# Stick-breaking attention weights as sigmoid(z) times a scanned product of sigmoid(-z), with the mask of a step ahead of the scan of the step before

## What is computed

```python
def sb_attend(q, k, v, q_pos, k_pos):
    z = jnp.einsum('bqhd,bkhd->bhqk', q, k).astype(jnp.float32) * SB_SCALE
    visible = (k_pos[None, :] < q_pos[:, None])[None, None]
    log_skip = jnp.where(visible, jax.nn.log_sigmoid(-z), 0.0)
    between = lax.cumsum(log_skip, axis=3, reverse=True) - log_skip
    weight = jnp.where(visible, jnp.exp(jax.nn.log_sigmoid(z) + between), 0.0)
    return jnp.einsum('bhqk,bkhd->bqhd', weight.astype(v.dtype), v)
```

## Time and profile before

| what | us |
|---|---|
| median of 3 runs | 846.8 (846.52 to 847.92) |
| the profiled execution | 848.45, its span 846.3 |
| PE busy | 798.5 (94% of the span) |
| DVE, ACT, POOL busy | 335.2, 244.5, 175.2 |
| stick-breaking stage, first scores to first scores of the sparse branch | 222.45 to 343.11 |
| experts | about 604 to the end |

### The profile page before, as it was taken

One profiled execution on the slowest core, in us unless ns is written; L12 is line 12 of the kernel. 1 busy time (PEld: TensorE's weight loads), 2 busy tenths in 40 slices (PEclk: granted clock), 3 DMA queues, 4 the chain that ended last, 5 costly groups with the idle time before them and its releaser, 6 DMA issues. The chain is left out here.

```text
span 846.3 us, 11854 instructions
## 1 busy us (share of the span) xinstructions
PE 798.5 (94%) x4611; PEld 495.2 (59%) x4611; DVE 335.2 (40%) x961; ACT 244.5 (29%) x492; POOL 175.2 (21%) x184
## 2 busy tenths in 40 slices
PE   7989999999989899999999999999899999999785
PEld 4465444688756557765666685555655555555452
DVE  5221564998245552444642255444621111111101
ACT  3031233102255554333333351121222222222211
POOL 2314450000132222000000001000233344333222
PEclk9999999999989999999999999999999999999998
DMA  8624020303300200204013089726799999999995
GB/s 270 197 100 127 8 100 1 119 36 137 117 1 2 79 21 8 100 0 149 1 27 74 1 338 404 271 100 223 249 367 398 395 396 403 395 398 397 401 405 147
DMA packets 59624, 155.80 MB, mean 184 GB/s; under 512 B 15464, under 2 KB 22088, under 8 KB 52400
## 3 DMA queue, kind: packets, MB, share of 16 engines
q1 hardware_dynamic: 50912, 141.75, 44.8%
q0 software_dynamic: 8656, 13.28, 5.9%
HBM read 147.38 MB, written 15.99 MB: 193 GB/s over the span
## 5 line engine op out<-in xcount | busy, mean ns | idle before, releaser
L857 PE MATMUL quad<-ring_w,xnT 128*128 128x512 f32 (+1 forms) x192 | 79.4, 554 | 0.0
L1059 PE MATMUL pair<-xnT,ring_w 128*128 128x272 f32 x256 | 69.8, 413 | 1.6 <-ACT tabs L1647 1.6
L1175 PE MATMUL pair<-xnT,ring_w 128*128 128x272 f32 x256 | 65.8, 403 | 0.0
L1904 POOL TENSOR_TENSOR arena<-arena 128x1024 f32<-128x1024 f32 (+5 forms) x18 | 29.6, 1645 | 168.9 <-DVE arena L2176 168.9
L1954 POOL DMA_INDIRECT out_y_prompt<-ring_w,idx x32 | 50.7, 1585 | 64.2 <-ACT ring_w L1813 63.6
L857 PE MATMUL quad<-xnT,ring_w 128*128 128x280 f32 (+1 forms) x256 | 60.6, 396 | 0.0
L1059 PEld LDWEIGHTS pair<-xnT,ring_w 128*128 128x128 f32 x256 | 47.2, 196 | 16.4 <-issue 5.9
L1175 PEld LDWEIGHTS pair<-xnT,ring_w 128*128 128x128 f32 x256 | 46.5, 189 | 14.7 <-issue 6.0
L857 PEld LDWEIGHTS quad<-xnT,ring_w 128*128 128x128 f32 x256 | 48.2, 190 | 10.8 <-issue 0.4
L857 PEld LDWEIGHTS quad<-ring_w,xnT 128*128 128x128 f32 x192 | 34.3, 189 | 31.7 <-issue 26.0
L1949 POOL DMA_INDIRECT ring_w<-xn_d,idx x32 | 33.1, 1036 | 94.3 <-PE quad L1421 45.3
(11 more groups left out here) (286 smaller groups left out, 1213.3 us busy)
## 6 DMA issues: line engine op xcount, KB each, us to landing
arena<-in_w_gate SPq DMA_DIRECT2D x21, 1024.0 KB, 22.4
arena<-in_w_up SPq DMA_DIRECT2D x21, 1024.0 KB, 25.1
arena<-in_w_down SPq DMA_DIRECT2D x40, 512.0 KB, 20.1
ring_w<-in_w_in SPq DMA_DIRECT2D x8, 2048.0 KB, 8.5
ring_w<-in_w_down SPq DMA_DIRECT2D x20, 512.0 KB, 21.7
xnT<-in_w_gate SPq DMA_DIRECT2D x4, 1024.0 KB, 19.2
xnT<-in_w_up SPq DMA_DIRECT2D x4, 1024.0 KB, 20.9
ring_w<-in_w_in SPq DMA_DIRECT2D x3, 1024.0 KB, 7.4
```

What stands on the lines that cost most here:

```text
L857: last = nc.tensor.matmul(o, l, r, start=i == 0, stop=i == len(mms) - 1)
L1059: last = nc.tensor.matmul(bank[6 + job % 2][:, 0:hi - lo], chunk8(6 + cb // 4)[:, k, c0:c0 + P], xT[:, k, lo:hi], start=k == 0, stop=k == ...
L1175: last = nc.tensor.matmul(bank[6 + job % 2][:, 0:hi - lo], w[:, k, c0:c0 + P], rhs[:, k, lo:hi], start=k == 0, stop=k == kt - 1)
L1904: nc.gpsimd.tensor_tensor(v, v, lb[:, i % LB, :, 0:SBJ[i]["n"]], ALU.subtract).then_inc(logw_ready, 1)
```

## The change

The weights are now made as a product. ACT makes sigmoid(-z) into `lb` and sigmoid(z) into `zb`, for the main jobs straight from PSUM; DVE scans `lb` as a running product; POOL multiplies `zb` by the product that is shifted by one key. The cap, the Ln and both Exps are gone. For the main jobs DVE only masks the diagonal block, in place in PSUM; for tail and sample it still copies z to `zb`. The scores of the next job now wait for the second sigmoid (`beta_ready`). In DVE's order the mask of job i stands ahead of the scans of job i-1. Each scan and each multiplication (one for each head) signals by itself. PE does filler portion A ahead of `values_weighed`, and the filler is dealt out otherwise: the products of portions A and B over the 21 iterations were 5+2, 6+2, 5+2, 4+2, 3+1, 2+1, then 5+2, 4+2, 3+1, 2+1 three times, 8+3, 8+3, 8+3; they are now 5+2, 8+4, 8+4, 8+3, 3+1, 2+1, the same three times, 6+2, 4+2, 4+1.

```diff
@@ filler_plan
-    weight = [max(0, SBJ[min(i, NSB - 1)]["n"] + 100) if i < NSB else 900 for i in range(NSB + 3)]
+    weight = [j["n"] + (500 if 1 <= i <= 3 else 100) for i, j in enumerate(SBJ)] + [700, 500, 400]
@@ PE
                 if i:
-                    pe.wait_ge(cap_ready, i)
+                    pe.wait_ge(beta_ready, i)
...
-                pe.wait_ge(w_ready, i + 1)
+                pe.wait_ge(w_ready, 2 * i + 2)
...
                 if i < NSB:
                     scores(i)
+                gate_products(GATE_FILL[i][0])
                 if i >= 3 and SBJ[i - 3]["ends"]:
                     values_weighed(i - 3)
-                gate_products(GATE_FILL[i][0])
@@ ACT
                     act.wait_ge(cap_ready, i + 1)
+                    z = zb[:, i % ZB, :, 0:n] if SBJ[i]["kind"] != "main" else \
+                        pairs[0].rearrange("p (u c) -> p u c", u=2)[:, :, 0:n]
                     if i >= LB:
-                        act.wait_ge(logw_ready, i - LB + 1)
-                    v = lb[:, i % LB, :, 0:n]
-                    link(nc.scalar.activation(v, zb[:, i % ZB, :, 0:n], ACT.Exp))
-                    nc.scalar.activation(v, v, ACT.Ln, bias=1.0).then_inc(ln_ready, 1)
-                gates_copied(gates_done(i - 1, 2))
-                if 0 <= i - 1 < NSB:
-                    act.wait_ge(logw_ready, i)
-                    w = zb[:, (i - 1) % ZB, :, 0:SBJ[i - 1]["n"]]
-                    nc.scalar.activation(w, w, ACT.Exp).then_inc(w_ready, 1)
+                        act.wait_ge(w_ready, 2 * (i - LB + 1))
+                    rest = nc.scalar.activation(lb[:, i % LB, :, 0:n], z, ACT.Sigmoid, scale=-1.0)
+                    rest.then_inc(rest_ready, 1)
+                    if i >= ZB:
+                        act.wait_ge(wT_ready, i - ZB + 1)
+                    if SBJ[i]["kind"] != "main":
+                        act.wait_ge(rest_ready, i + 1)
+                    nc.scalar.activation(zb[:, i % ZB, :, 0:n], z, ACT.Sigmoid).then_inc(beta_ready, 1)
+                gates_copied(gates_done(i, 1))
                 if i >= 3 and SBJ[i - 3]["ends"]:
...
                     nc.scalar.activation(dst, src, ACT.Copy).then_inc(acc_free, 1)
-                gates_copied(gates_done(i, 1))
@@ POOL
-                pool.wait_ge(scan_ready, i + 1)
-                v = zb[:, i % ZB, :, 0:SBJ[i]["n"]]
-                nc.gpsimd.tensor_tensor(v, v, lb[:, i % LB, :, 0:SBJ[i]["n"]], ALU.subtract).then_inc(logw_ready, 1)
+                pool.wait_ge(beta_ready, i + 1)
+                for u in range(2):
+                    pool.wait_ge(scan_ready, 2 * i + u + 1)
+                    n = SBJ[i]["n"]
+                    v = zb[:, i % ZB, u, 0:n - 1]
+                    nc.gpsimd.tensor_tensor(v, v, lb[:, i % LB, u, 1:n], ALU.mult).then_inc(w_ready, 1)
@@ DVE
+            def suffix_sums(i):
+                dve.wait_ge(rest_ready, i + 1)
+                for u in range(2):
+                    n = SBJ[i]["n"]
+                    v = lb[:, i % LB, u, 0:n][:, ::-1]
+                    nc.vector.tensor_tensor_scan(v, v, none_more.broadcast_to([P, n]), 1.0, ALU.mult, ALU.add)\
+                        .then_inc(scan_ready, 1)
+
             for i, j in enumerate(SBJ):
                 dve.wait_ge(z_ready, i + 1)
-                if i >= ZB:
+                if i >= ZB and j["kind"] != "main":
                     dve.wait_ge(wT_ready, i - ZB + 1)
...
+                if j["kind"] == "main":
+                    z = whole[:, :, n:n + P]
+                    ins = nc.vector.tensor_tensor(z, z, seen.rearrange("p (o c) -> p o c", o=1).broadcast_to([P, 2, P]), ALU.min)
+                else:
+                    nc.vector.tensor_copy(zb[:, i % ZB, :, 0:n], whole[:, :, 0:n])
+                    for u in range(2):
+                        ins = nc.vector.tensor_tensor(zb[:, i % ZB, u, n:n + DEC], bank[3 - u][:, 0:DEC], seen32, ALU.min)
                 ins.then_inc(cap_ready, 1)
                 next(first_selection, None)
-                dve.wait_ge(ln_ready, i + 1)
...
+                if i:
+                    suffix_sums(i - 1)
                 next(first_selection, None)
+            suffix_sums(NSB - 1)
```

More of the change, by code:

```diff
@@ L60 @@
 HIDDEN = float(np.float32(-3.0e38))
-Z_CAP = 30.0
 TAKEN = float(np.float32(-3.2e38))
@@ L472, in build @@
         cap_ready = sem("cap_ready")
-        ln_ready = sem("ln_ready")
+        rest_ready = sem("rest_ready")
         scan_ready = sem("scan_ready")
-        logw_ready = sem("logw_ready")
+        beta_ready = sem("beta_ready")
         w_ready = sem("w_ready")
@@ L2159, in _ @@
                     dve.wait_ge(wT_ready, i - ZB + 1)
                 whole = pairs[0].rearrange("p (u c) -> p u c", u=2)
-                width = P if j["kind"] == "main" else DEC
-                n = j["n"] - width
-                if n:
-                    nc.vector.tensor_scalar(zb[:, i % ZB, :, 0:n], whole[:, :, 0:n], Z_CAP, None, ALU.min)
-                for u in range(2):
-                    if j["kind"] == "main":
-                        z, mask = whole[:, u, n:n + P], seen
-                    else:
-                        z, mask = bank[3 - u][:, 0:DEC], seen32
-                    ins = nc.vector.scalar_tensor_tensor(zb[:, i % ZB, u, n:n + width], z, Z_CAP, mask, ALU.min, ALU.min)
+                n = j["n"] - (P if j["kind"] == "main" else DEC)
@@ L2172, in _ @@
                 next(first_selection, None)
-                dve.wait_ge(ln_ready, i + 1)
-                for u in range(2):
-                    v = lb[:, i % LB, u, 0:j["n"]][:, ::-1]
-                    ins = nc.vector.tensor_tensor_scan(v, v, none_more.broadcast_to([P, j["n"]]), 0.0, ALU.add, ALU.add)
-                ins.then_inc(scan_ready, 1)
+                if i:
+                    suffix_sums(i - 1)
                 next(first_selection, None)
+            suffix_sums(NSB - 1)
             for _ in first_selection:
```

## The result

The changed kernel takes **834.33 us** (median of 4 runs, 832.52 to 839.32), the kernel before 847.36 (846.52 to 848.57) beside it. The ratio is 0.9853, with a 95% interval of 0.9828 to 0.9879: 1.5% faster, 13.0 us against the forecast 15.7. It lies inside the range, 3.2 us above the forecast: 2.7 by which the gain is smaller, and 0.5 because the kernel before, run beside it, took 847.36 and not 846.8. The profiled execution took 835.87, 1.5 above the median; the other three took 832.52, 832.79 and 839.32.

A forecast was written before the change was run, and what follows sets the result against it. PE, busy for 94% of the span, was taken to bound the kernel. 9.0 us less idle and 6.7 us of clock regained make 15.7, so 846.8 - 15.7 = 831.1 us, with 80% inside 828.8 to 839.5.

The forecast's parts named there:

- What bounds the stage, and what goes: In the changed stage PE idles 9.0 us less and the slow clock's 6.7 us come back, together 15.7 us.
- Who takes the waits away: Ahead of values_weighed, portion A's three calls, about 1.5 us, cover most of the 1.99 wait; ACT's shorter work the rest.
- PE's work at full clock: Stage's 120.66 us less 10.65 idle and 6.7 slow clock leaves 103.3 us, which nothing in the change makes less.
- The score banks: Next scores wait for the second sigmoid: 2.2 us after 384-key scores, against 3.17 when PE needs them; 1.0 to spare.
- The weights: Mask, scans, then POOL behind both scans: 512-key weights after 6.0 us against 7.6, 384-key after 9.9 against 10.5.
- list of signs: Signs expected in the new profile, among them a stage 105 us long and POOL's halves starting when the second scan ends.
- The filler copies: In iterations 1 and 2 ACT copies filler results behind both sigmoids: a wait of 0.6 us, bounds 0 and 1.6.
- Start and end: At the stage's start PE waits 0.4 to 0.5 us for ACT's first activations; at the end 0.5 for its last copies.
- The table loads: Two more ACT loads, 1.28 us each, cost nothing, covered by idle time; rival with both exposed: 833.7 us, 15%.
- The gain lost later: Rival: up to half the gain is lost to the experts' loads, bound by DMA engines: 839 us or more; chance 6%.
- The rival on the slower side: Rival: each of 16 main jobs stalls about 0.9 us at the score banks: 852 us; chance 5%.
- The chain of 838: Rival: scan or POOL slower, 512- and 384-key jobs late by 1 to 1.5 us per group: about 838 us; chance 15%.

The follow-up runs named there:

- the first eight of the experiments: Kernel before with portion A moved, also with new shares; new arithmetic alone; changed kernel with value products first, old shares, old scan order, one or two extra sigmoids: 832.26 to 847.44 us.
- the four kernels above: Changed kernel 834.33 us; the same with value products first 834.49; with old shares 833.79; new arithmetic with all old orders 832.26.
- twelve traces above: Kernels without eight-matmul filler, stage's end to span's end: 504.9 to 505.8 us in five with the first or 31st expert at lower clock, 502.3 to 504.1 in seven.
- the filler did not settle it: Extra matmuls in waits ahead of experts 26 to 30: eight on the changed kernel 842.58 us, eight on the new arithmetic alone 841.68, two on the changed kernel 833.69.

## Why the prediction was right, and where it was off

**What bounds the stage, and what goes.** Right. The stage was forecast at 120.66 - 15.7 = 105.0 and took 105.68. The waits ahead of the value products went, and all of the slow clock's 6.7 us with them (in the profiled execution). That 1.99 once left the clock alone did not mean that something else made it fall: with waits of 0.84 at most in the main jobs it stayed at 1.00 behind 240, in the changed kernel and the first eight of the experiments.

**Who takes the waits away.** Half right. The prediction gave most of it to portion A and the rest to the shorter work of ACT. As a sum that fits: portion A alone leaves 0.42 to 0.71 of 1.99. But the arithmetic alone takes all of it too, and so the parts do not add: 11.7 us of stage for the one, 16.2 for the other, 15.0 for all. Either takes away most of the waits and the fall of the clock with them, and little is left for the other: PE idles 4.3 us with the moved line alone and 1.4 with the arithmetic alone.

**PE's work at full clock** (term 103.3 us). Mis-sized, and the reason of the 0.7 us. The prediction said that nothing in the change makes it less, and did not ask whether something makes it more. It is 104.26: 0.75 for the place of portion A and 0.42 for the shares, by the four kernels above. With neither it is 103.09, so the 103.3 itself was right to 0.2.

**The score banks** (2.2 against 3.17). Right to 0.1: 2.17 measured, 1.0 to spare. The mask takes 0.43, forecast 0.5; sigmoids from PSUM take 1.02 and 0.81, on the line of Exp and Copy, as taken.

**The weights** (6.0 against 7.6, spare 1.6; 9.9 against 10.5, spare 0.6). The price was too high, and the order right only in part. From 268.87 the weights of 512 keys are done after 5.1, 7.7 is when they are wanted; those of 384 keys (277.15) after 8.3 against 10.6. The spares are 2.6 and 2.3. The mis-sized term is POOL's: it ends 1.9 us after the two scans (274.00 against 272.07), where 2.54 were taken, two halves of 1.27. Alone a half takes 1.09, and the first one does not start when the second scan ends, as the prediction's list of signs had it, but 0.97 before. Nor do the scans of 384 keys wait for POOL, as the sum has it: they start at 273.53, 0.47 before POOL is done, and take 2.13 for it where 1.81 were taken. The running product costs what the running sum did, 2.34 for two of 512.

**The filler copies** (0.6, bounds 0 and 1.6): 0.37. The prediction left open what makes it: with the old shares the wait is 0, and with one more sigmoid it is 2.5.

**Start and end** (0.4 to 0.5, and 0.5): 0.51 and 0.53.

**The table loads** (nothing). Right, both lie in idle time of ACT. The drain of the Trainium skill ("ScalarE: Activation LUTs", What ACT_TABLE_LOAD costs), by which this would have been 836.4, does not show in time: 1.65 and 2.07 us of waiting for DVE still stand behind the loads. Nor does it show at 488.79 in the kernel before, where no wait covers the load: the activation behind it starts 1.29 after it.

**The gain lost later** (6%, up to half of it). It came true in small. The three terms of 2.6 us stand above. The first two are delays of PE where it meets a transfer or a copy, and they also go the other way: over the kernel before, the changed one and the first eight of the experiments (the ten kernels up to the two superfluous sigmoids) the distance from the stage's end to the 31st expert is 477.7 to 480.7 us. The 1.5 us of clock is in this one execution. At the lower clock some expert's matmuls (L1429, 5.1 to 5.4 us) stand in six of these ten executions. At the experts in between a later wait can hide them. At the 31st, behind which no expert waits, nothing does, and at the first it seems not to be hidden either: in the two of the ten where it is slow the distance is 480.6 and 480.7, in the others 479.6 at most. So of the 3.5 us by which this span is above its forecast (834.1 against 830.6), 0.7 are the stage, 0.15 is ahead of it, and 2.6 behind it. For the median, 3.2 above, the stage's 0.7 is shown, and 0.5 comes from the kernel before, which was that much slower beside it; that other executions lose the remainder in the experts as well is an inference. The comparison of twelve traces above fits it, the filler did not settle it.

**The rival on the slower side** (decides at 0.8 us more for each sigmoid). Its point was right, its place only in part. Two superfluous sigmoids are 1.4 us for a main job on average ((2.04 + 1.62 + 1.19 + 0.77) / 4), 0.7 for each of the two, and land level with the kernel before. But only six of 16 jobs stall, for 0.76 on average, where 16 times 0.9 was the picture; more is lost at the start, at the filler copies and in the clock behind them, and 3.6 us of the median is not in this trace. The chain of 838 did not come: nowhere does PE wait for POOL.

## What to carry to other kernels

Where an engine is busy for nine tenths of a stage, two remedies for the same wait do not add: work out what each leaves of the wait alone, and keep the cheaper one. Here one moved line gives 11.7 of the 15.0 us of stage, and the new arithmetic without the moves on PE and DVE gives 16.2. Fill work moved into a gap has a price of its own, in the busy time of the engine that it fills (0.4 and 0.75 us here) and in the buffers that its results need (4.5 us with the old arithmetic).

## What the hardware showed that I had not expected

- TensorE's busy time for the same matmuls at a granted clock of 1.00 depends on their order: 103.09 to 104.26 us for the same 712 records. A group of filler, value products and transposes takes 0.15 us more than the same one with the value products first.
- Behind a wait of 2.84 us near the stage's start the granted clock was 0.68 for 5.3 us, while it stayed at 1.00 behind waits of 1.58 to 1.63 at about the same place in three kernels.
- GpSimd's half of the product, started 0.97 us before the end of a scan on VectorE, has a record of 1.85 us and not 1.09; the pair ends 0.35 us earlier than one that starts when the scan is done. Two scans on VectorE that start 0.82 us before GpSimd is done take 2.48 and not 1.81.
- A product of 128x511 on GpSimd takes 1.09 us where the subtraction of two heads of 128x256 took 1.27: halves of 127, 255, 383 and 511 take 0.41, 0.65, 0.86 and 1.09, that is 0.18 and 1.78 ns an element, so 1.27 is the price of one piece of 512 and 0.18 once more for the second piece. That it is the second piece fits these numbers; no run varied it alone, and the two are different operations.
- A float32 matmul of 128x256 with 128 rows and 128 columns of weights leaves two records of 0.226 us each, while a record of the experts' matmuls of the same width, with 64 columns of weights, takes 0.115.
